# Hybrid encoder block: the mixer put into one TensorE order, modulation rows transposed on chip

## The reference

```python
mod = silu(c) @ w_ada + b_ada                 # 6*D: sh1, sc1, g1, sh2, sc2, g2
h = rmsnorm(x, norm1_g) * (1 + sc1) + sh1
proj = h @ w_in                               # [pool | q | k | v | g], 1024 each
# A: pool. 4 groups of 256 channels, windows 2, 4, 8, 16:
pooled = window_sum / count - u               # count is smaller at the two ends
pool_out = (pooled @ pool_w[group]) * pool_scale
# B: retention, 4 heads of 256, rotary q and k, chunks of 128 tokens, both directions:
ret = (q k^T * decay) v  +  q_decay * (q @ state_fwd)  +  q_decay_b * (q @ state_bwd)
state = state * chunk_decay + (k * k_decay)^T v
ret_out = silu(g) * ret / rms(ret)            # rms over the head's 256 channels
x = x + g1 * (concat(pool_out, ret_out) @ w_out)
h2 = rmsnorm(x, norm2_g) * (1 + sc2) + sh2
x = x + g2 * ((silu(h2 @ w_gate) * (h2 @ w_up)) @ w_down)      # d_ff = 5632
out = rmsnorm(x, final_g)
```

## Time and profile before

| | |
|---|---|
| median of 3 runs | 3463.46 us (3450.49 to 3469.59) |
| the profiled execution | 3454.59 us, span of its slowest core 3453.0 us |
| spans of the 8 cores | 3411.1 to 3453.0 us |
| TensorE busy | 2960.8 us, 86% of the span |
| VectorE, ScalarE busy | 875.3 us (25%), 605.7 us (18%) |
| stages 1, 2, 3 | to 234 us, to 397 us, to 1325 us |
| stages 4 and 5 | to the end |

### The profile page before, as it was taken

One profiled execution on the slowest core, in us unless ns is written; L12 is line 12 of the kernel. 1 busy time (PEld: TensorE's weight loads), 2 busy tenths in 40 slices (PEclk: granted clock), 3 DMA queues, 4 the chain that ended last, 5 costly groups with the idle time before them and its releaser, 6 DMA issues.

```text
span 3453.0 us, 40495 instructions; the slowest of 8 cores (3411.1 to 3453.0 us)
## 1 busy us (share of the span) xinstructions
PE 2960.8 (86%) x14944; PEld 1449.1 (42%) x14944; DVE 875.3 (25%) x1650; ACT 605.7 (18%) x1231; POOL 204.3 (6%) x388
## 2 busy tenths in 40 slices
PE   1449468658787885996999999999999999999998
PEld 1324135334454553443444444444444444444443
DVE  0236432423425433662001012101120101210112
ACT  1322203304215042432000001000010000100001
POOL 0010000000000000000000000000000000000000
PEclk8679788787897978998999999999999999999999
DMA  9859479589552516668997469995499964999742
GB/s 195 184 100 145 107 119 131 103 125 132 98 112 55 117 50 194 212 227 173 212 173 162 171 151 214 174 169 182 142 197 188 171 185 147 169 205 172 161 158 93
DMA packets 130849, 533.17 MB, mean 154 GB/s; under 512 B 35456, under 2 KB 69472, under 8 KB 73184
## 3 DMA queue, kind: packets, MB, share of 16 engines
q0 software_dynamic: 55040, 388.52, 60.4%
q1 hardware_dynamic: 75616, 142.07, 12.7%
HBM read 768.00 MB, written 81.84 MB: 246 GB/s over the span
## 4 chain that ended last, share of the span: by engine, by line
PE 77%; DMA 16%; DVE 3%; issue 2%; ACT 1%; SPq 1%; DVEq 0%; POOL 0%; ACTq 0%; POOLq 0%
PE ps L1073 35%; PE ps L1145 17%; PE ps L540 10%; PE ps L944 6%; DMA arena<-b_ada 5%; PE ps L841 3%; DMA catT<-arena 3%; DMA arena<-cs 3%; PE ps L738 2%; DMA arena<-invc 1%; PE ps L354 1%; PE ps L1156 1%; DMA arena<-modrows 1%; DMA arena<-wsc 1%; DMA arena<-h2d 1%
## 5 line engine op out<-in xcount | busy, mean ns | idle before, releaser
L1073 PE MATMUL ps<-arena 128*128 128x512 bf16 x5632 | 1219.2, 380 | 31.1 <-DMA arena<-h2d 27.0
L1073 PEld LDWEIGHTS ps<-arena 128*128 128x128 bf16 x5632 | 551.6, 98 | 697.5 <-issue 35.2
L540 PE MATMUL ps<-arena 128*128 128x512 bf16 x2048 | 463.5, 390 | 150.1 <-DVE arena L710 102.9
L1145 PE MATMUL ps<-arena 128*128 128x512 bf16 x2640 | 570.5, 379 | 0.0
L1080 DVE TENSOR_TENSOR arena<-ps,arena 128x512 bf16<-128x512 f32 x176 | 121.4, 691 | 1058.8 <-PE ps L1073 1058.0
L1145 PEld LDWEIGHTS ps<-arena 128*128 128x128 bf16 x2640 | 258.3, 98 | 311.5
L540 PEld LDWEIGHTS ps<-arena 128*128 128x128 bf16 x2048 | 203.3, 100 | 406.4 <-issue 180.2
L1078 ACT ACTIVATE arena<-ps 128x512 f32<-128x512 f32 x176 | 104.7, 597 | 1035.7 <-PE ps L1073 1032.6
L944 PE MATMUL ps<-arena 128*128 128x512 bf16 x1024 | 225.0, 381 | 25.4 <-DMA arena<-catT 22.3
L1092 DVE TENSOR_TENSOR arena<-ps,arena 128x512 f32<-128x512 f32 x64 | 43.9, 686 | 514.6 <-PE ps L1145 501.1
L944 PEld LDWEIGHTS ps<-arena 128*128 128x128 bf16 x1024 | 99.8, 98 | 144.2 <-issue 27.9
(11 more groups left out here) (106 smaller groups left out, 1677.4 us busy)
## 6 DMA issues: line engine op xcount, KB each, us to landing
arena<-wsc POOLq DMA_DIRECT2D x88, 1024.0 KB, 5.2
arena<-w_gate POOLq DMA_DIRECT2D x88, 1024.0 KB, 17.5
arena<-w_up POOLq DMA_DIRECT2D x88, 1024.0 KB, 20.6
arena<-w_ada POOLq DMA_DIRECT2D x48, 1024.0 KB, 18.2
arena<-x SPq DMA_DIRECT2D x32, 1024.0 KB, 9.7
arena<-w_in POOLq DMA_DIRECT2D x20, 1024.0 KB, 25.8
wsc<-w_down POOLq DMA_DIRECT2D x20, 1024.0 KB, 43.4
arena<-cs SPq DMA_DIRECT2D x64, 256.0 KB, 3.4
```

The source lines that it names most:

```text
L540: ins = e.matmul(PS[bank][:, :], lhsT=slab[:, kc, fc * 128:(fc + 1) * 128], rhs=hT[:, kc, tt * 512:(tt + 1) * 512], start=(kc == 0), stop= ...
L1073: ins = e.matmul(PS[bank][:, :], lhsT=slab[:, kc, jj * 128:(jj + 1) * 128], rhs=hb[:, kc, :], start=(kc == 0), stop=(kc == KC - 1))
L1145: ins = e.matmul(PS[bo + m][:, :], lhsT=actT[:, j, m * 128:(m + 1) * 128], rhs=slab[:, a, :], start=(j == 0), stop=(j == NFC - 1))
```

## The change

- Stage 1: `mod_slab` is a generator of two steps. The row is copied out by ScalarE, and in the next step two float32 matmuls with one column each turn its two halves into columns of `modT`; VectorE adds the bias from `bT`, loaded once. No per-slab DMA and no read-back of `modrows`; only rows 2 and 5 are written, each once at the end of stage 3.
- The two barriers are gone. New buffers over old memory name the buffers whose place they take (`Buf.over`), and their first writer waits for those.
- `invc` is replaced by a constant factor with 16 corrected columns (`edge`). The decay tables are computed ahead of the pool. The `pool_w` loads stand ahead of the first `w_in` slab on POOL.
- Stages 2 and 3 are one loop. `producers()` gives 160 steps, each one projection group; after each step one round of `consumers()` is emitted (pool sums and matmuls, `bchain`, `outs`), two in every eighth step from step 48 on. Projection groups use banks 0 to 2 (was 0 to 3), pool matmuls 4 to 7, k transposes 7, state deltas 6, scores 4, outputs 5. Bank 3 holds the transposes of the outputs and the modulation slabs. Rotary evictions are 512 wide. The forward state sweep is part of the output rounds, with 3 forward states kept in place of 16.
- `mod_step()` is called in 2 of 5 steps from step 48 on, and after each round of the last `outs`.
- `mod_slab` no longer calls `precast`; the jobs that the 20 `w_in` slabs leave are issued after the loop.

```diff
-        if True:
-            c0 = v * D + cb * 256
-            slab, bs = load_w(w_ada[c0 // 256], 4096, v3(256))
-            if v >= 2:
-                precast(1)
...
-            sc.dma("sp", d_brow[j], brow[j], b_ada[0:1, c0:c0 + 256], writes=[B_brow[j]])
...
+    def mod_slab(v, cb, bank, c0, pb):
+        slab, bs = load_w(w_ada[v * 8 + cb])
...
+        sc.op("pe", fn, reads=[bs, B_cact], writes=[pb])
+        sc.op("act", lambda e: e.activation(out=mrow[j], in_=PS[bank][0:1, c0:c0 + 256], func=AF.Copy),
+              writes=[pb, B_mrow[j]])
+        yield
+
+        def fn2(e):
+            ins = None
+            for i in range(2):
+                ins = e.matmul(PS[bank][:, c0 + i:c0 + i + 1], lhsT=mrow[j][0:1, i * 128:(i + 1) * 128], rhs=onef[0:1, 0:1],
+                               start=True, stop=True)
+            return ins
+        sc.op("pe", fn2, reads=[B_mrow[j], B_small], writes=[pb])
...
-    sc.barrier(skip=("pool",), skip_dsems=(d_pre,))
...
+    for g_ in range(4):
+        sc.dma("pool", d_pw[g_], pw[:, g_], pool_w[g_].rearrange("(cc p) d -> p cc d", p=128), writes=[B_pw])
...
-        bank = abank[0] % 4
+        bank = abank[0] % 3
...
+            sc.op("dve", lambda e, cur=cur, up=up, po=po, w=w: e.scalar_tensor_tensor(
+                out=po, in0=cur[:, 8:8 + S], scalar=1.0 / w, in1=up[:, 8:8 + S], op0=ALU.mult, op1=ALU.subtract), reads=[curB, Bu], writes=[Bp])
...
+    def bchain(h):
+        prev = None
+        for n in list(range(NCH - 1, 0, -1)) + [None]:
+            if prev is not None:
+                k_delta(h, prev[0], prev[1], "b", prev[0] == NCH - 1)
+            prev = None if n is None else (n, k_tr(h, n, 4 + h))
+            yield
...
+            sc.op("pe", ftr, reads=[B_retn[p], B_small], writes=[PB[3]])
+            sc.op("dve", lambda e: e.tensor_tensor(out=rstg[r4], in0=PTb[3][:, 0:256].rearrange("p (a b) -> p a b", b=128),
+                                                  in1=sgT[:, :, ns], op=ALU.mult),
+                  reads=[B_sg[n // 4]], writes=[PB[3], B_rstg[r4]])
+            sc.dma("sp", d_rstg[r4], catT[8 + 2 * h:10 + 2 * h, :, ns].rearrange("c p t -> p c t"), rstg[r4],
+                   reads=[B_rstg[r4]], writes=[B_cat[8 + 2 * h], B_cat[9 + 2 * h]])
+
+        for r in range(NCH + 2):
+            if r < NCH - 1:
+                k_delta(h, r, fj[0], "f", r == 0)
+            if r < NCH - 2:
+                fj[0] = k_tr(h, r + 1, h)
+            if r < NCH:
+                scores(r)
+            if 0 <= r - 1 < NCH:
+                outmm(r - 1)
+            if 0 <= r - 2:
+                outtr(r - 2)
+            yield
...
+    def producers():
+        for gi in (3, 2, 1, 0):
+            yield from pool_steps(gi)
+            produced.add(("p", gi))
+        for h in range(NH):
+            yield from k_steps(h)
+            yield from v_steps(h)
+            produced.add(("kv", h))
+            yield from q_steps(h)
+            yield from g_steps(h)
+            produced.add(("qg", h))
...
+    mod_jobs = [mod_slab(v, cb, 3, 0, PB[3]) for v in (2, 3, 4, 5) for cb in range(8)]
...
+    for i, _ in enumerate(producers()):
+        next(cons, None)
+        if i >= 48:
+            assert "pool" in produced
+            if (i - 48) % 5 in (0, 2):
+                mod_step()
+            if i % 8 == 7:
+                next(cons, None)
+    for _ in cons:
+        mod_step()
+    while mstate[0] < len(mod_jobs):
+        mod_step()
+    mod_row(2)
...
     precast(len(pre_jobs))
     for b_ in B_wsc:
         b_.w = (d_pre.h, d_pre.val)
```

More of the change, by code:

```diff
@@ L29, in __init__, with over @@
         self.r = {}
+        self.pre = ()
+    def over(self, *old):
+        self.pre = tuple(old)
+        return self
 class DSem:
@@ L464, in build_nc @@
         xload(m)
-    rounds = pipeline_rounds([p1_gen(m) for m in range(NCH)], 3)
-    mods01 = [mod_gen(0, 7), mod_gen(1, 7)]
-    sc_pp = ar.alloc((KC,), F32)
-    B_pp = Buf("pp")
-    for i in range(max(NCH + 4, 16)):
+    d_misc = [sc.dsem(f"dmisc{i}") for i in range(4)]
+    sc.dma("sp", d_misc[0], bT.rearrange("p a b -> p (a b)"), b_ada, writes=[B_bT])
+    sc.dma("sp", d_misc[1], g1n_sb, g1n, writes=[B_gn])
+    p1 = [p1_gen(m) for m in range(NCH)]
+    mods = [mod_slab(i // 8, i % 8, 6 + i % 2, 0, PB[6 + i % 2]) for i in range(16)]
@@ L544, in inproj_group, with pool_steps @@
         return bank
-    def w_in_slab(c0):
-        r_ = load_w(w_in[c0 // 256], 4096, v3(256))
-        precast(1)
-        return r_
-    def pool_gen(gi):
-        g2 = gi % 2
-        L = S + 16
+    pool_units = {}
+    def pool_steps(gi):
         slab, bs = w_in_slab(gi * 256)
-        if gi == 1:
-            for g_ in range(4):
-                sc.dma("pool", d_pw, pw[:, g_], pool_w[g_].rearrange("(cc p) d -> p cc d", p=128), reads=[B_fence2], writes=[B_pw])
-        sc.dma("sp", d_invc[g2], invc_sb[g2], invc[gi], writes=[B_invc[g2]])
@@ new lines, in build_nc, with nb @@
+    rstg = [ar.alloc((2, 128), BF16) for _ in range(4)]
+    junk3 = ar.alloc((DH,), BF16)
+    peak3 = ar.off
+    def nb(name):
+        return Buf(name).over(*(old1 + oldp))
+    B_qT = [nb(f"qT{t}") for t in range(4)]
+    B_sg = [nb(f"sg{t}") for t in range(4)]
+    B_Sb = [nb(f"Sb{n}") for n in range(NCH)]
+    B_Sf = [nb(f"Sf{i}") for i in range(3)]
+    B_S32 = {d_: nb("S32" + d_) for d_ in "fb"}
+    B_kdt = [nb("kdt0"), nb("kdt1")]
+    B_PTm = [nb("PTm0"), nb("PTm1")]
+    B_qfb = [nb("qfb0"), nb("qfb1")]
@@ new lines, in consumers @@
+    def consumers():
+        for gi in (3, 2, 1, 0):
+            while ("p", gi) not in produced:
+                yield
+            yield from pool_cons(gi)
+        produced.add("pool")
+        for h in range(NH):
+            while ("kv", h) not in produced:
+                yield
+            yield from bchain(h)
+            while ("qg", h) not in produced:
+                yield
+            yield from outs(h)
+    mod_jobs = [mod_slab(v, cb, 3, 0, PB[3]) for v in (2, 3, 4, 5) for cb in range(8)]
```

686 lines of the change are left out of this document (318 added, 368 removed).

## The result

The changed kernel takes 3538.97 us (median of 4 runs, 3524.3 to 3615.72) against 3459.47 us: ratio 1.0215, 95% interval 1.0166 to 1.0264. It is slower; whether by more than 2% these runs leave open. In one of the four (3615.72 us) one die ran at a lower granted clock, and the ratio leaves it out. The profiled execution took 3538.3 us (span 3536.8), 213 us above the 3325 that the sum gave for it.

What follows compares the result with a forecast made beforehand. It saw some 360 us of idle time or slow clock in the mixer's 1093 us, with the feed-forward full on TensorE. 1326.8 became 1192, plus 6: 129 us off 3454.6 gives 3325, forecast 3330, range 3225 to 3415.

Steps and rivals of the forecast that it cites:

- Part 1: Up to the first projection: transfers hold stage 1, POOL waits for `pool_w`; first projection at 196 us, 38 us won.
- Part 2: Steps 0 to 47, pool and first head's k and v: 169 + 14 us, 20 for stores, end at 399.
- Part 3: Steps 48 to 159: 520 us of dense work and waits of 60, 15 and 50; 645 us, end at 1044.
- the doubled rounds: Steps 48 to 159: the second round of a step starts inside the first's 3.5 us; 15 us, bounds 0 and 30.
- VectorE's order stalls every step and not every fifth: A sign, named beforehand, that would show the forecast wrong, about stalls from VectorE's order of work; no size given.
- Bank 3: Output rounds of steps 48 to 159: modulation steps make TensorE wait for VectorE's product; 60 us taken.
- `cs`: DMA queues in steps 48 to 159: `cs` loads and stores meet a full software queue; 50 us, bounds 0 and 114.
- Part 4: Tail after step 160: 12 conversions take 87 us, stores left 8, row 4; last modulation row written at 1192 us.
- Part 5: Behind the barrier: no `w_out` slab can load ahead; 6 us more, bounds 0 and 10, nothing changes after.
- The store chain becomes the wall: Rival, SP in the output rounds: each of a head's 16 stores lands after 13 us; slower, 3609 us, chance 5%.
- The clock: Rival, steps 48 to 159: small stalls hold the granted clock at 0.62, 520 us become 839; 3649 us, chance 4%.
- my own case: The whole kernel by the main sum: 3330 us, covering 3265 to 3395, with clock 0.88 to 0.95; chance 58%.

Runs made afterwards that it cites:

- run 5: The changed kernel with the 12 left-over conversions issued among the gate and up slabs of the feed-forward's first quarter; 3513.7 and 3539.8 us, no interval.
- run 12: 10 with modulation steps in 3 of 5 steps and the consumer round emitted ahead of the rotary eviction; 3299.7 us, ratio 0.9551.
- 6: run 5 with the modulation step ahead of the consumer round; 3458.4 us, ratio 1.0009.
- run 2: The changed kernel with each `catT` store writing a Buf of its own, so stores don't wait for each other; 3514.0 and 3503.5 us, no interval.
- run 8: run 7 with stores that don't wait for each other and the two modulation row stores issued early; 3398.0 us, ratio 0.9828.
- run 7: 6 with each `cs` piece asked for two rotary tiles ahead; 3443.2 us, ratio 0.9963.
- 9: run 8 with the 12 conversions behind modulation slabs in the middle, in place of the feed-forward; 3366.1 us, ratio 0.9763.
- 10: run 8 with one conversion behind each of the first 12 `w_out` tiles, in place of the feed-forward; 3360.5 us, ratio 0.9768.

## Why the prediction was wrong

The interleaving does pay what the sum said it would, and more, but not in this order of emission and not with what it leaves over. By the steps of the prediction:

**Part 1** came out right (193.1 for 196), and POOL was seen waiting for `pool_w`, but two errors cancel in it: POOL reached the first `w_in` slab at 180.2 us and not at 187, and the slab landed after 12.6 us and not after 8.6. **Part 2** was 27 us short: three stores of the pool took 20.17, 18.98 and 8.19 us on the chain between 249 and 297 us, at a DMA share of 0.97. That is 47 us for a term of 20 with a bound of 40. The "half the price" for half the rows was wrong.

**Part 3 failed in two terms.** The sum 520 + 60 + 15 + 50 became 753 by about 592 busy and 161 idle. (1) The dense work was priced at rows near the upper level of 2.4 GHz, with 27 us for the clock in the range only. The granted clock was 0.85 over 423 to 1100 us, and the busy time is 72 us above the price. Some 15 to 25 of these are core 2's own: the median core of the same execution is busy for 577 us up to its last projection, and that of run 5, with the same order of work and 0.89 or 0.90 on all cores, for 566, which still is 46 above the price. How much of that is the clock, and how much the small matmuls, wasn't measured. (2) The state chain behind the rotary eviction, 48.8 us, stood in "the doubled rounds" as 15 with a bound of 30; run 12 shows that it is an emission order and not VectorE's load, since the same work in another order waits 17.7 us. The sign that was named for it, "VectorE's order stalls every step and not every fifth", did not come: it is 20 waits in 112 steps, but each of 2.4 us and a chain of its own, which the sum did not have. Bank 3 (48.7 for 60) and `cs` (54.4 for 50) were sized right. But the waits of bank 3 cost more than their length: between runs 5 and 6 the median core gains 57 us with 36 us less idle time.

**Part 4 failed where it says that the tail's rounds are not what ends last and that the stores meanwhile "land one in about 13 us".** The conversions started 39 us after part 3's end (42 predicted), but with the slab ahead of them took 115 us for 94 (7 and 87), 9.1 us for each MB of the queue against 7.5 (115 by 12.60). Stores took 20 us in the mean in that time, and since each holds a staging buffer, TensorE's rounds wait for them: 41 us of rounds were left for a term of 8 us. The row took 22.19 for 4. Runs 2, 5 and 8 show each piece: on the median core, the last state matmul comes 54 us earlier with free stores, `w_out` 80 us earlier without conversions, and 53 us earlier with both stores and rows freed. The Trainium skill (DMA: Bandwidth & Descriptors, Queues, rings and completion order) has a DMA engine alternate between queues packet by packet, which, with each row of a store counted as one packet, gave an estimate of 12 us a store. The six stores of 1215 to 1330 us land after a median of 23.8 us, so by that rule alone the price comes out at half.

**Part 5** was right at the start (31 for 34), but its term of 6 us was too small. From the barrier to the last `w_out` matmul it takes 251.3 us before (1326.8 to 1578.1) and 266.7 in the changed kernel (1394.6 to 1661.3), 15 us more: before, matmuls ran from 1340.1 on while the last slab still landed, and now the first starts at 1425.6, at the end of the 31 us. That behind this nothing changes was right: 1874.9 and 1875.5 us.

**The rivals.** "The store chain becomes the wall" named the mechanism, but in the middle at 13 us a store; it was the tail at 20. "The clock" did not come: over 423 to 1100 us the cores have 0.85 to 0.90, by the lower end of the 0.88 to 0.95 that my own case expected, and not 0.62. So the loss was in no rival as it was written; it is made of terms of my own case. The range ended at 3415 because it left out most of the case in which terms reach their bounds. Even all bounds together, 3483, are 56 us under the measured 3539: they allow the middle 750 us (753 measured) and the tail 176 (218 measured).

**Left open.** In the changed kernel cores 2 and 3 show a mean granted clock of 0.77 from 474 to 640 us, where the other six have 0.89 to 0.92 in the same program; core 2 is the slowest core. Cores 6 and 7 of run 7 and cores 2 and 3 of run 8 show the same in their middles (0.90 for 0.92 to 0.94, 0.88 and 0.89 for 0.93 and 0.94). No run tells why. Nor was a place found where the 12 conversions cost nothing: on the median core 47 us in the middle (9 against 8), 52 in the `w_out` stage (10 against 9, behind its first matmul), 75 to 77 in the first quarter. In the tail, with chained stores and late rows, it was 80.

## What to carry to other kernels

When engines run fixed lists, price a merged order by asking for every operation what stands ahead of it on its own engine and who waits for it in turn: two moves of single lines (modulation before the round, round before the rotary) were worth 1.6% each by the ratios, some 55 us, and the first alone takes back three quarters of the loss. Read what a move is worth on several cores: the slowest one of the changed kernel had 22 us of its own. Count what a removed issuing place leaves over, and where it lands: 12 conversions of about 9 us each stood right ahead of a barrier. And don't chain small stores, or a row of 4-byte pieces, behind bulk casts: a store cost 20 us there and 1.64 us with the queue empty.

## What was not expected of the hardware

- A 64 KB store on the hardware queue takes 14 to 26 us while the software queue fills the DMA engines to 95%, more than the 16.09 us of the earlier trace rows.
- 12 conversions from float32 to bfloat16 between two places in memory run at 9.1 us an MB (with one slab among them); the mixed traffic of the earlier trace rows had 6.3 to 7.4.
- A modulation row of 4-byte pieces takes 22.19 us to write at a DMA share of 0.24, and 45.13 us in run 2, where it follows the conversions.
- Two row transposes in float32 (four matmul records of one column each) take 0.60 us even between full-speed groups, for 0.4 taken.
- Stalls of 2 to 6 us cost more than their length. Between runs 5 and 6 about 40 us of bank 3's waits go, the idle time falls by 36 us, and the last projection comes 57 us earlier on the median core; the granted clock up to there rises from 0.90 to 0.92. In run 12, with 57 us idle up to the last projection, it is 0.96.
